# Router logits as fp32 products, wider band scores, and seven TensorE products nobody reads

## The reference

```python
# banded attention (C): queries of chunk n see the keys of chunks n-1 and n, 64 tokens each
scores = einsum('bnqhgd,bnkhd->bnhgqk', qc, band(k)) * HEAD_DIM ** -0.5   # 8 q heads, 2 kv heads
# every sub-layer
h = normalize(x) * (1.0 + scale) + shift
x = layer_norm(ALPHA * x + (1.0 + gate) * f(h), ln_g, ln_b)
# f in the channel mixer of layer 1
logits = h @ w_router + b_router                      # (256, 1024) @ (1024, 8)
top_logit, top_idx = top_k(logits, 2)
top_w = softmax(top_logit)
# for each expert e, on the rows that chose it:
y += top_w * ((silu(h @ w1[e]) * (h @ w3[e])) @ w2[e])
```

## Time and profile before

| | us |
|---|---|
| median of three runs | 1831.04 |
| profiled execution | 1830.93 |
| its span | 1829.0 |
| PE busy | 1691.5 (92%) |
| DVE busy | 1390.1 (76%) |
| ACT busy | 1022.6 (56%) |
| mean granted TensorE clock | 0.966 |

### The profile page before, as it was taken

How to read it: one execution, slowest core, us unless ns; L and a number is a source line. 1 busy time by engine, 2 the same in 40 slices (tenths; PEclk the granted TensorE clock), 3 DMA queues, 4 the chain that set the end, 5 groups by cost and what they waited for, 6 DMA issues and landing times.

```text
span 1829.0 us, 21282 instructions
## 1 busy us (share of the span) xinstructions
PE 1691.5 (92%) x7548; PEld 1319.1 (72%) x7549; DVE 1390.1 (76%) x1192; ACT 1022.6 (56%) x817; POOL 36.7 (2%) x40
## 2 busy tenths in 40 slices
PE   1999899999999859989999989999999999999995
PEld 0587758887778737767877768888777777787773
DVE  7685868676776876887887875566588788788887
ACT  0464333433555325766767755545477677676772
POOL 1100010000100000000000000000000000000000
PEclk9998999999999978999999999999999999999998
DMA  9884459773774346997998975666599899899991
GB/s 346 316 308 155 136 178 339 276 252 138 272 259 162 107 146 224 384 371 266 366 352 307 379 291 194 219 226 210 183 374 389 296 380 376 307 369 339 326 392 75
DMA packets 210529, 502.21 MB, mean 275 GB/s; under 512 B 9137, under 2 KB 13409, under 8 KB 210481
## 3 DMA queue, kind: packets, MB, share of 16 engines
q1 hardware_dynamic: 208770, 496.15, 75.4%
q0 software_dynamic: 1712, 5.43, 1.0%
HBM read 500.50 MB, written 1.05 MB: 274 GB/s over the span
## 4 chain that ended last, share of the span: by engine, by line
PE 80%; DVE 12%; issue 6%; ACT 1%; DMA 0%; POOL 0%; DVEq 0%; SPq 0%; ACTq 0%; POOLq 0%
PE ps L1382 21%; PE ps L1384 20%; PE ps L1383 20%; DVE w_lo L1257 4%; PE ps L1393 4%; PE ps L1388 3%; PE ps L1389 3%; PE ps L1801 2%; PE ps L1916 2%; PE ps L1841 1%; DVE mod_acc L882 1%; PE ps L1508 1%; DVE stats L904 1%; DVE gates L1059 1%; DVE w_lo L857 1%
## 5 line engine op out<-in xcount | busy, mean ns | idle before, releaser
L1257 DVE TENSOR_TENSOR w_lo<-w_raw,w_hi 128x2048 fp32r<-128x2048 f32 x333 | 757.8, 2290 | 213.0 <-ACT w_hi L738 210.9
L738 ACT CAST w_hi<-w_raw 128x2048 fp32r<-128x2048 f32 x333 | 634.5, 1910 | 237.9 <-PE ps L1384 151.4
L1382 PE MATMUL ps<-w_hi,actT_hi 128*128 128x512 f32 (+1 forms) x1464 | 585.0, 400 | 30.9 <-DVE w_lo L1257 16.6
L1384 PE MATMUL ps<-w_hi,actT_lo 128*128 128x512 f32 (+1 forms) x1464 | 569.6, 389 | 0.0
L1383 PE MATMUL ps<-w_lo,actT_hi 128*128 128x512 f32 (+1 forms) x1464 | 569.2, 389 | 0.0
L1382 PEld LDWEIGHTS ps<-w_hi,actT_hi 128*128 128x128 f32 x1464 | 278.4, 190 | 103.9 <-DVE w_lo L1257 27.5
L1384 PEld LDWEIGHTS ps<-w_hi,actT_lo 128*128 128x128 f32 x1464 | 278.1, 190 | 57.5
L1383 PEld LDWEIGHTS ps<-w_lo,actT_hi 128*128 128x128 f32 x1464 | 278.9, 190 | 54.5 <-issue 2.4
L857 DVE TENSOR_TENSOR w_lo<-w_raw,w_hi 128x2048 fp32r<-128x2048 f32 x81 | 185.4, 2290 | 96.9 <-ACT w_hi L491 96.7
L491 ACT CAST w_hi<-w_raw 128x2048 fp32r<-128x2048 f32 x81 | 154.3, 1909 | 117.7 <-PE ps L1384 102.1
L1388 PE MATMUL ps<-w_hi,gT_hi 128*128 128x512 f32 x336 | 140.0, 417 | 14.7 <-DVE gT_hi L1284 14.7
(11 more groups left out here) (251 smaller groups left out, 1274.4 us busy)
## 6 DMA issues: line engine op xcount, KB each, us to landing
w_raw<-in_exp_w_dram SPq DMA_DIRECT2D x336, 1024.0 KB, 6.5
w_raw<-in_ffn_w_dram SPq DMA_DIRECT2D x33, 1024.0 KB, 5.4
w_raw<-in_w_mod_mix_dram SPq DMA_DIRECT2D x24, 1024.0 KB, 8.3
w_raw<-in_w_mod_ffn_dram SPq DMA_DIRECT2D x24, 1024.0 KB, 5.3
w_raw<-in_w_gate_dram SPq DMA_DIRECT2D x24, 1024.0 KB, 7.4
w_raw<-in_w_in_dram SPq DMA_DIRECT2D x14, 1024.0 KB, 7.6
w_raw<-in_w_out_dram SPq DMA_DIRECT2D x8, 1024.0 KB, 5.1
w_raw<-in_w_branch_c_dram SPq DMA_DIRECT2D x4, 1024.0 KB, 5.1
```

The costliest lines, as they stand in the source:

```text
L738: nc.scalar.copy(w_hi[:, i % SPLIT, :], w_raw[:, i % RING, :]).then_inc(split_hi, 1)
L1257: TTn(w_lo[:, i % SPLIT, :], w_raw[:, i % RING, :], w_hi[:, i % SPLIT, :].bitcast(F32), ALU.subtract).then_inc(piece_used, 1)
L1382: MM(to, hi, w_h, start=first, stop=False)
L1384: return MM(to, lo, w_h, start=False, stop=last)
```

## The change

1. **Band scores.** For tile 0, one product of 128 columns for each head instead of three of 64; for tile 1, one of 128 columns and one of 64.
2. **Logits.** Instead of rounding `h` and the router's weights, ACT copies the transposed `h` out as it is (`actT_raw`), and PE multiplies it, as stationary operand, with `w_rt` in fp32: 8 products of 8 columns for each tile, straight into the layout that DVE reads. Tile 0's come before tile 1 is transposed.
3. **Order.** For this sub-layer, `norms` becomes `route_norms`: DVE takes the residual and the statistics of tile 1 before it modulates tile 0; ACT rounds the expert pieces 0, 1, 2 and `h` in between; PE sends the gate rows ahead of the transposes of tile 0; DVE makes `h_lo` of tile 1 behind the choice.
4. **Unread products.** PE runs four fp32 products of 512 columns into a free PSUM bank behind the logits, and three behind the position counts (`stay_busy`).
5. `h_hi` and `h_lo` swap their places in SBUF; two small tiles and some semaphores go.

```diff
@@ band_scores
-    MM(ps[:, 4 + par, i * P:i * P + CHUNK], cT[rows, i, q0:q0 + P], key(2 * t), start=True, stop=True)
-    MM(ps[0:CHUNK, 4 + par, i * P + CHUNK:(i + 1) * P], cT[rows, i, q0:q0 + CHUNK], key(before), start=True, stop=True)
-    ins = MM(ps[CHUNK:P, 4 + par, i * P + CHUNK:(i + 1) * P], cT[rows, i, q0 + CHUNK:q0 + P], key(2 * t + 1), start=True, stop=True)
+    ins = MM(ps[:, 4 + par, i * P:(i + 1) * P], cT[rows, i, q0:q0 + P], keys(2 * t, 2), start=True, stop=True)
+    if t:
+        ins = MM(ps[0:CHUNK, 4 + par, i * P + CHUNK:(i + 1) * P], cT[rows, i, q0:q0 + CHUNK], keys(2 * t - 1, 1),
+                 start=True, stop=True)
@@ ACT, layer 1, behind the mixer
+def route_norms(sub, n, held, ahead):
+    def high_h(t):
+        A(h_hi[:, t, :], hbuf[:, t, :], ACT.Copy).then_inc(hh_ready, 1)
+    root(n + 1, 0)
+    ahead(0)
+    root(n + 2, 0)
+    ahead(1)
+    root(n + 3, 1)
+    keep_gate(sub, held)
+    keep_turned(sub, 0, held)
+    high_h(0)
+    root(n + 4, 1)
+    ahead(2)
+    keep_turned(sub, 1, held)
+    high_h(1)
...
-A(w_rt_hi[:, :, :], w_rt[:, :, :], ACT.Copy).then_inc(rt_hi, 1)
-for t in range(TT):
-    ins = A(h_hi[:, t, :], hbuf[:, t, :], ACT.Copy)
-act.wait_ge(logitsT_sent, 1)
-A(place[0:EXPERTS, 0, :], ps[0:EXPERTS, ROUTE, 0:SEQ], ACT.Copy).then_inc(logitsT_ready, 1)
@@ DVE, the same place
+def route_norms(chain, sub, n, free, f, f_done, n_ln):
+    dve.wait_ge(gate1_ready, sub)
+    f_done(0)
+    residual(chain, f, 0)
+    statistics(chain, hbuf, 0)
+    dve.wait_ge(ln_loaded, n_ln)
+    inverse_std(chain, n + 1, 0)
+    chain.step(layer_norm(chain, 0))
+    statistics(chain, x, 0)
+    f_done(1)
+    residual(chain, f, 1)
+    dve.sem_inc(rows_read, 1)
+    statistics(chain, hbuf, 1)
+    inverse_std(chain, n + 2, 0)
+    dve.wait_ge(mod_sent, sub + 1)
+    modulate(chain, 0, free)
+    inverse_std(chain, n + 3, 1)
+    chain.step(layer_norm(chain, 1))
+    statistics(chain, x, 1)
+    inverse_std(chain, n + 4, 1)
+    modulate(chain, 1, free)
+    dve.sem_inc(x_ready, 1)
...
-TTn(w_rt_lo[:, :, :], w_rt[:, :, :], w_rt_hi[:, :, :].bitcast(F32), ALU.subtract).then_inc(rt_lo, 1)
-for t in range(TT):
-    ins = TTn(h_lo[:, t, :], hbuf[:, t, :], h_hi[:, t, :].bitcast(F32), ALU.subtract)
+low_h(0)
 rest_of_piece(EXPERT, 0, sbase + MIX.n_split)
...
 TTn(gap, m2, m1, ALU.subtract).then_inc(gap_ready, 1)
+low_h(1)
 dve.wait_ge(e2_ready, 1)
@@ PE, layer 1
+send_gate(3, 4)
 h_transposed(layer * 2 + 1, 0, 4)
...
-send_gate(3, 4)
+pe.wait_ge(rt_loaded, 32)
+logits(0)
 second_tile(3, 4)
-for k in range(KD):
-    ins = product(ps[0:EXPERTS, ROUTE, 0:SEQ], w_rt_hi[:, k, :], w_rt_lo[:, k, :], actT_hi[:, k, :], actT_lo[:, k, :],
-                  k == 0, k == KD - 1)
-pe.wait_ge(logitsT_ready, 1)
...
+logits(1).then_inc(logits_sent, 1)
+def stay_busy(products):
+    for _ in range(products):
+        MM(bank(3), ident, cst[:, C_BAND:C_BAND + BANK], start=True, stop=True)
+stay_busy(4)
 pe.wait_ge(sel_ready, 1)
...
     MM(to[:, 16:24], ones, sel[:, 1, :], start=False, stop=True).then_inc(pos_sent, 1)
-pe.wait_ge(hh_ready, 1)
-pe.wait_ge(hl_ready, 1)
+stay_busy(3)
+pe.wait_ge(hh_ready, TT)
+pe.wait_ge(hl_ready, TT)
```

More of the change, by code:

```diff
@@ L256, in trunk @@
         ffn = ExitStack()
+        h_lo = sb("h_lo", [P, TT, D], F32R, scope=ffn)
         h_hi = sb("h_hi", [P, TT, D], F32R, scope=ffn)
-        h_lo = sb("h_lo", [P, TT, D], F32R, scope=ffn)
         yacc = sb("yacc", [P, TT, D], scope=ffn)
@@ L277, in trunk @@
         ps = ctx.enter_context(nc.psum_tensor("ps", [P, 8, BANK], F32))
-        gT_end_hi, gT_end_lo = (h_lo[:, part, 0:BANK].rearrange("p (b c q) -> p b c q", b=2, q=P) for part in range(2))
+        gT_end_hi, gT_end_lo = (h_hi[:, part, 0:BANK].rearrange("p (b c q) -> p b c q", b=2, q=P) for part in range(2))
         assert 2 * DENSE_PANELS[-1] == BANK
@@ L514, in keep_gate, with keep_turned @@
                 ins.then_inc(gate1_ready, 1)
[L516 to L522, removed]
+            def keep_turned(sub, t, held):
                 for c in range(2):
@@ L531, in turned_h, with norms @@
                     A(actT_hi[at], actT_raw[at], ACT.Copy).then_inc(hT_hi_ready, 1)
-            def norms(sub, n, free, held, keep_h, ahead=None):
+            def norms(sub, n, held):
                 root(n + 1, 0)
                 root(n + 2, 0)
-                keep_h(sub, 0, held)
+                turned_h(sub, 0, held)
                 root(n + 3, 1)
@@ L541, in norms @@
                 root(n + 4, 1)
[L542 to L545, removed]
+                turned_h(sub, 1, held)
+            def route_norms(sub, n, held, ahead):
[13 more added lines that the diff above has]
+                high_h(1)
             act.wait_ge(c_loaded, 16)
@@ L938, in modulate @@
                     STT(part, part, rstd[:, t:t + 1], bank(free + c), ALU.mult, ALU.add).then_inc(h_ready, 1)
[L940 to L946, removed]
             def rest_of_turned(sub, t, met, count):
@@ L954, in rest_of_turned, with norms @@
                     TTn(actT_lo[at], actT_raw[at], actT_hi[at].bitcast(F32), ALU.subtract).then_inc(hT_lo_ready, 1)
-            def norms(chain, sub, n, free, held, f, f_done, n_ln):
+            def norms(chain, sub, n, free, f, f_done, n_ln):
                 dve.wait_ge(gate1_ready, sub)
@@ L1134, in _ @@
                        lambda: rest_of_turned(layer * 2, 1, split_used, sbase + SPLIT + SPLIT))
-                norms(chain, layer * 2 + 1, layer * 8 + 2, 0, 4, lambda t, c: bank(4 + 2 * t + c),
+                (route_norms if layer else norms)(chain, layer * 2 + 1, layer * 8 + 2, 0, lambda t, c: bank(4 + 2 * t + c),
                       lambda t: dve.wait_ge(split_used, sbase + (MIX.n_split + SPLIT)) if t else dve.wait_ge(out_sent, layer + 1),
@@ L1176, in _ @@
                            lambda: rest_of_turned(1, 1, split_used, MIX.n_split + SPLIT + SPLIT))
-                    norms(chain, 2, 6, 4, 0, lambda t, c: bank(2 * t + c),
+                    norms(chain, 2, 6, 4, lambda t, c: bank(2 * t + c),
                           lambda t: dve.wait_ge(split_used, LAYER_SPLITS + SPLIT) if t else dve.wait_ge(y_sent, 1), 64)
@@ L1195, in _ @@
                     dve.wait_ge(logits_sent, 1)
-                    step(TTn(logit, ps[:, ROUTE + 1, LOGITS:LOGITS + 16].rearrange("p (t e) -> p t e", t=TT), b_rt[:, :].unsqueeze(1).broadcast_to(wide), ALU.add))
+                    step(TTn(logit, ps[:, LOGITS, 0:16].rearrange("p (t e) -> p t e", t=TT), b_rt[:, :].unsqueeze(1).broadcast_to(wide), ALU.add))
                     def largest(values, m, is_it):
@@ L1673, in _ @@
                     after(j)
+                if layer:
+                    send_gate(3, 4)
                 h_transposed(layer * 2 + 1, 0, 4)
@@ L1768, in _, with logits @@
                 else:
[L1769 to L1782 removed]
+                    def logits(t):
+                        for c in range(2):
+                            pe.wait_ge(hT_raw_ready, 12 + 2 * t + c + 1)
+                            for k in range(4 * c, 4 * c + 4):
+                                ins = MM(ps[:, LOGITS, t * EXPERTS:(t + 1) * EXPERTS], actT_raw[:, k, t * P:(t + 1) * P], w_rt[:, k, :],
+                                         start=k == 0, stop=k == KD - 1)
+                        return ins
+                    pe.wait_ge(rt_loaded, 32)
+                    logits(0)
+                    second_tile(3, 4)
+                    logits(1).then_inc(logits_sent, 1)
[3 more added lines that the diff above has]
+                    stay_busy(4)
                     pe.wait_ge(sel_ready, 1)
```

41 lines of the change are left out of this document (12 added, 29 removed).

## The result

The changed kernel took 1804.78 us (median of four runs, 1803.92 to 1806.65); the kernel before took 1829.39 in the same job. The ratio is 0.9868, with a 95% interval of 0.9846 to 0.989: 1.3% faster. The profiled execution took 1806.65, its span is 1804.6, 24.4 us less than before. TensorE still bounds the kernel.

A forecast was written before the change was run, and what follows sets the result against it. TensorE was taken to bound the kernel, with 80% of the chain. The mixer's 11.8 us and 10.4 from norms, choice of experts and the clock behind made 22 off 1830.93: 1809 us, range 1800 to 1821.

The forecast's parts named there:

- tile 0 with its clock, two layers: Band scores, tile 0, both layers: wide products save 8.2 us, and half of the lost clock comes back, 3.9.
- tile 1 with its clock: Band scores, tile 1: no change from the new products; a third of the lost clock comes back, 1.7 us.
- waited away by ACT and DVE: Mixer: ACT and DVE make later pieces behind the same attention steps, so some TensorE lead is lost, 2 us.
- norms: Norms before the experts: DVE stands 2.3 us for TensorE's last product of tile 1; net 0.5 us later.
- logits, after the norms' loss: Choice of experts: with fp32 logit products the logits stand at 671.1 instead of 679.84, 8.7 us earlier.
- up to the positions: Choice of experts: the five position products are done at 678.0 instead of 684.9, a gain of 6.9 us.
- up to X: Choice of experts through the gather: the first expert product comes at 687.0, 9.6 us earlier.
- clock behind X: Behind the first expert product: the clock may fall again, low for 4.5 us instead of 6.2; gain 0.8.
- mixer clock as before: Rival, chance 0.20: the mixer's clock falls as before and only shapes pay there; 16.6 us gained, 1814 us.
- First fills: Four unread products behind the logits: the clock rises after 4.5 us and they end at 676.8, 3.0 late.
- my own rival with the fills at 1.2 GHz: Rival, chance 0.15: the unread products run at 1.2 GHz throughout; the choice gives 1.4 us, the whole 13.2, 1818 us.
- Slower by an expert's form: Rival, chance 0.02: differently rounded logits move a token; one expert going from 128 to 129 tokens costs 80 us, 1890.

The follow-up runs named there:

- e5: The changed kernel with wide band-score products at tile 0 alone and the old three 64-key products a head at tile 1; 1819.42 us.
- e11: The kernel before with only the changed band scores, keeping its old router; 1815.43 us.
- e10: The kernel of e5 with thirty-two unread products added at the program's start, which move the later code; 1803.81 us.
- e2: The changed kernel with tile 1's band scores as eight 64x128 products, then eight 64x64 products, instead of alternating; 1790.65 us.
- e1: The changed kernel with the old three 64-column band-score products a head back in both token tiles; 1817.4 us.
- e6: The changed kernel with DVE modulating tile 0 before it adds tile 1's residual in the norms before the experts; 1803.98 us.
- e3: The changed kernel without its seven unread products; 1805.87 us.
- e4: The changed kernel with three more unread 512-column products right behind expert 0's gather; 1806.12 us.
- e9: The changed kernel with sixteen more unread products at the program's start, which move the later code; 1823.44 us.

## Why the prediction was right, step by step

The time (1804.8 for 1809, range 1800 to 1821) and the places were right. Four sizes were off: tile 0 by +4.0 us, tile 1 by -3.8, what is waited away by +2, and the choice with the clock behind it by -0.2. That the first two nearly cancel is luck. The rows for the logits, the positions and X are each counted from the mark, so each holds the one above it and the norms.

| step | forecast | measured, us gained |
|---|---|---|
| tile 0 with its clock, two layers | 8.2 + 3.9 | 16.1 |
| tile 1 with its clock | 0 + 1.7 | -2.1 |
| waited away by ACT and DVE | -2 | 0 |
| norms | -0.5 | -0.4 |
| logits, after the norms' loss | 8.7 | 8.8 |
| up to the positions | 6.9 | 7.0 |
| up to X | 9.6 | 10.1 |
| clock behind X | 0.8 | about 0.1 |

- *Tile 0.* Eight heads in 1.09 us, under my 1.7: the nearest row was an alternation of pairs, and this is one run of a single shape. From the scores of tile 0 to those of tile 1 it is 23.7 us in each layer instead of 31.8 and 31.7. The heads are 4.7 of these 8.0, so the clock behind them gave 3.3 a layer, not the half of 3.9 that I took: with the fall gone, the pool products behind the scores too ran at 2.4 GHz. I had counted the idle microsecond behind them as a reason for it to fall; in layer 1 it is still there (11.11 busy of 12) and the clock stayed. The rival "mixer clock as before" fell with that.
- *Tile 1.* The mis-sized term of the wrong sign. I left shapes at no change and gave a third of its clock back. A head went from 0.62 (the old form, read in `e5`) to 0.67, and the clock stayed low 6.7 us in layer 1 instead of 3.4. The second is most of the 2.1, and it is no fixed price of the form: with the same new products `e11` was low for 3.5, and with the same old ones `e10` took 1.4 us less from the scores to the mark than `e5` (485.8 against 487.2), its clock behind tile 1 of layer 0 low for half as long. `e2` shows that grouping, not columns, was what it lacked.
- *Waited away.* Nothing: in `e1` and `e11` the lead at the mark comes through to X in full. No row spoke for the 2 us.
- *Norms.* DVE stood 2.26 us for PE's last product, forecast 2.3, and the second half of tile 1's modulation begins 650.58 - 624.96 = 25.6 us behind the mark, before 25.2; `e6` shows that the wait was on the path.
- *Logits.* 656.68 - 653.24 = 3.4 us of fp32 products at 1.2 GHz, as forecast. The first step of the choice came 8.8 us earlier counted from the mark.
- *First fills.* The clock rose 4.6 us after they began (forecast 4.5); they ended at 662.5, and DVE stood 1.92 us behind them. `e3` confirms what I could only price: their delay and their gain nearly cancel. My "5 us at most hang on them" had no sum behind it, and my own rival with the fills at 1.2 GHz priced 10.4 - 1.4 = 9.0; `e3` measures 1.1 at X.
- *Clock behind X.* It did fall again, ahead of X, and stayed low to about 678.4, 6.0 us behind X where I had 4.5 and the kernel before 6.2: a gain of 0.1. `e4` removes it, and shows why the whole term was worth nothing: ACT comes into the loop too late to use it.
- *The end.* "The experts' loop waits for its loads" did not come; their 1132 us are the same before and after. That was not assured: `e9` shows that the same change, with its code elsewhere, would have measured 0.3% instead of 1.3%. My rivals had no such case; that the time fell into the range rested on luck in the place of the code. The kernel before is such a place too: it has the stand of the earlier trace rows, and its 1132.4 us from X to the end are 4.4 more than the 1128.0 of `e10`.
- *Slower by an expert's form.* The experts' steps are the same, 210.0 us for expert 3 as before.

## What to carry to other kernels

Group TensorE's small products by their shape in the array: one run of a shape each was worth 13 us here that fewer and wider products alone did not give. Feeding an idle engine to keep its clock pays only if the next engine in line is ready to use what it wins; look at who is late at the first real product. Before believing a gain or a loss of 1% in a kernel with branches, compare the stretches that the edit did not touch, and move the code once.

## What the runs showed of the hardware that I had not expected

- The same experts took from 1128.0 to 1147.1 us, and 15 of these 19 are the place of TensorE's code (`e9` against the changed kernel, `e10` against `e5` 18); counts of 7504 matmuls gave 1146.4 and 1147.1, of 7568 gave 1128.3, 1128.0, 1128.0.
- ACT stood 8.4 to 9.9 us between its last instruction ahead of the experts' loop and its first in it, and a table load of 1.28 comes on top.
- A change of shape cost about 0.26 us here. The clock fell in or right behind each row of them; with 16 products of one shape in 1.09 us it stayed at 2.4 GHz.
- From the first scores to the mark kernels with the same code agree within 0.2 us (489.3 to 489.5 in six with the changed scores and router, 503.3 in both with the old scores) where the clock falls for as long in all; where it does not, they differ by 1.2 to 1.4 (488.1 in `e11`; 487.2 and 485.8 in `e5` and `e10`). The first scores come between 134.0 and 138.0.
